# Opening layer 0 with half of the contraction: input products over half of K placed between the ada sums, gate sums behind q, rotary angles on GpSimd

## The reference

```python
mod = c_act @ w_ada[layer] + b_ada[layer]            # 6 x 1024 values
shift_m, scale_m, gate_m, shift_f, scale_f, gate_f = split(mod, 6)
h = rms_norm(x, g_mix) * (1.0 + scale_m) + shift_m
proj = h @ w_in                                      # 1024 x 1952
c_q, c_kv, k_rope, q_sb, k_sb, v_sb = split(proj)    # 256, 128, 32, 512, 512, 512
```

## Time and profile before

| | us |
|---|---|
| median of 3 runs (lowest, highest) | 1446.91 (1445.17, 1450.16) |
| the profiled execution, its time | 1443.41 |
| its span | 1441.6 |
| PE busy in the span | 1358.2 (94%) |
| DVE busy | 1261.1 (87%) |
| ACT busy | 937.8 (65%) |

### The profile page before, as it was taken

How to read it: one execution, slowest core, us unless ns; L and a number is a source line. 1 busy time by engine, 2 the same in 40 slices (tenths; PEclk the granted TensorE clock), 3 DMA queues, 4 the chain that set the end, 5 groups by cost and what they waited for, 6 DMA issues and landing times.

```text
span 1441.6 us, 18313 instructions
## 1 busy us (share of the span) xinstructions
PE 1358.2 (94%) x7090; PEld 1140.5 (79%) x7090; DVE 1261.1 (87%) x1141; ACT 937.8 (65%) x875; POOL 3.8 (0%) x35
## 2 busy tenths in 40 slices
PE   2899889999999879999999999999999999999995
PEld 2777789998987758887788888888888888888884
DVE  6878789887767778999999999989999989999997
ACT  1545443333437257887787878877787877878784
POOL 1000000000000000000000000000000000000000
PEclk9898999999899899999999999999999999999999
DMA  8973468997553129999999999999999999999992
GB/s 327 358 260 133 146 246 314 334 314 255 171 216 119 59 103 396 397 398 398 397 401 395 395 396 397 400 400 389 385 400 397 396 405 391 381 396 398 399 400 102
DMA packets 189596, 467.24 MB, mean 324 GB/s; under 512 B 8734, under 2 KB 10940, under 8 KB 175164
## 3 DMA queue, kind: packets, MB, share of 16 engines
q1 hardware_dynamic: 189500, 465.98, 86.2%
HBM read 464.90 MB, written 1.05 MB: 323 GB/s over the span
## 4 chain that ended last, share of the span: by engine, by line
PE 80%; DVE 8%; DMA 8%; ACT 3%; issue 1%; SPq 0%; DVEq 0%; ACTq 0%
PE bank L1596 16%; PE bank L1597 16%; PE bank L1598 16%; PE bank L1993 6%; PE bank L1994 6%; DMA raw<-in_w_ex_down 4%; PE bank L2036 3%; PE bank L2038 3%; PE bank L2012 3%; DMA raw<-in_w_ex_up 2%; DVE w_lo L1264 2%; DVE ring_sum L993 1%; PE bank L1639 1%; PE bank L1617 1%; PE bank L1939 1%
## 5 line engine op out<-in xcount | busy, mean ns | idle before, releaser
L1264 DVE TENSOR_TENSOR w_lo<-raw,w_hi 128x2048 fp32r<-128x2048 f32 x202 | 455.8, 2287 | 33.8 <-ACT w_hi L578 33.0
L578 ACT ACTIVATE w_hi<-raw 128x2048 fp32r<-128x2048 f32 x202 | 382.1, 1917 | 51.8 <-DMA raw<-in_w_ex_up 18.4
L554 ACT ACTIVATE w_hi<-raw 128x2048 fp32r<-128x2048 f32 (+1 forms) x54 | 102.3, 1897 | 131.2 <-PE bank L1598 118.4
L1264 DVE TENSOR_TENSOR fifth_lo<-raw,fifth_hi 128x2048 fp32r<-128x2048 f32 x67 | 153.2, 2287 | 11.9 <-ACT fifth_hi L578 11.4
L1264 DVE TENSOR_TENSOR more_lo<-raw,more_hi 128x2048 fp32r<-128x2048 f32 x67 | 153.2, 2287 | 11.3 <-ACT more_hi L578 11.0
L578 ACT ACTIVATE fifth_hi<-raw 128x2048 fp32r<-128x2048 f32 x67 | 128.4, 1916 | 22.7 <-DMA raw<-in_w_ex_gate 8.0
L578 ACT ACTIVATE more_hi<-raw 128x2048 fp32r<-128x2048 f32 x67 | 128.4, 1916 | 17.9 <-DMA raw<-in_w_ex_up 6.8
L922 DVE TENSOR_TENSOR w_lo<-raw,w_hi 128x2048 fp32r<-128x2048 f32 (+1 forms) x54 | 121.7, 2258 | 19.4 <-ACT w_hi L554 19.1
L1596 PE MATMUL bank<-h_hi,w_hi 128*128 128x256 f32 x448 | 128.1, 286 | 1.6 <-DVE gate_m L971 1.6
L1597 PE MATMUL bank<-h_lo,w_hi 128*128 128x256 f32 x448 | 126.7, 283 | 0.0
L1598 PE MATMUL bank<-h_hi,w_lo 128*128 128x256 f32 x448 | 126.7, 283 | 0.0
(11 more groups left out here) (344 smaller groups left out, 2834.7 us busy)
## 6 DMA issues: line engine op xcount, KB each, us to landing
raw<-in_w_ex_gate SPq DMA_DIRECT2D x112, 1024.0 KB, 11.9
raw<-in_w_ex_up SPq DMA_DIRECT2D x112, 1024.0 KB, 12.1
raw<-in_w_ex_down SPq DMA_DIRECT2D x112, 1024.0 KB, 12.9
raw<-in_w_ada SPq DMA_DIRECT2D x48, 1024.0 KB, 6.7
raw<-in_w_in SPq DMA_DIRECT2D x12, 1024.0 KB, 6.6
raw<-in_w_ff_gate SPq DMA_DIRECT2D x10, 1024.0 KB, 5.9
raw<-in_w_ff_up SPq DMA_DIRECT2D x10, 1024.0 KB, 5.9
raw<-in_w_ff_down SPq DMA_DIRECT2D x10, 1024.0 KB, 6.3
```

Source lines behind the costliest of these rows:

```text
L554: act_e.activation(w_hi[:, s % SPLIT, 0:words], raw[:, n % RAW, 0:words], ACT.Copy).then_inc(hi_done, 1)
L578: act_e.activation(dst, raw[:, (N0 + n) % RAW, :], ACT.Copy).then_inc(hi_done, 1)
L1264: dve.tensor_tensor(lo, raw[:, (N0 + n) % RAW, :], hi.bitcast(F32), ALU.subtract).then_inc(lo_done, 1)
```

## The change

The first eight ada units are no longer one block. Rows are now built in the order chunk 0 and chunk 2 (shift and gain of the first half of K), then chunks 1 and 3 (the second half). Only the first two rows (four units) stand ahead of the first weights. From layer 0's `w_in`, the first half of K comes for latents, v, q and k, with the four units of the other two rows between them; then the second half for latents, v and q, two gate units, `w_uq`, the second half of k, `w_ukv`, three units. ACT brings the second half of the transposed rows out unmodulated (`late_rows`) and modulates it in place later. Both wide sums for the gate stand behind the `w_ukv` product, in banks 4 and 5. `positions` is loaded ahead of the weights and the angles are made on POOL by 21 instructions. The biases of the gates are loaded later (in front of the 18th unit). Layer 1 keeps its order.

```diff
-    chunks = [(0, c) for c in range(12)] + [(1, c) for c in (0, 1, 2, 3, 6, 7, 8, 9, 4, 5, 10, 11)]
+    chunks = [(0, c) for c in (0, 2, 1, 3, *range(4, 12))] + [(1, c) for c in (0, 1, 2, 3, 6, 7, 8, 9, 4, 5, 10, 11)]
...
-    for u in ada_units[:8]:
-        add_ada(*u)
...
+        if l == 0:
+            for u in ada_units[:4]:
+                add_ada(*u)
+            add_half(w_in[l], 0, LAT, 0)
+            add_half(w_in[l], LAT + 2 * SW, SW, 0)
+            add_ada(*ada_units[4])
+            add_half(w_in[l], LAT, SW, 0)
+            add_ada(*ada_units[5])
+            add_half(w_in[l], LAT + SW, SW, 0)
+            add_ada(*ada_units[6])
+            add_ada(*ada_units[7])
+            add_half(w_in[l], 0, LAT, 1)
+            end(("lat", l), "split")
+            add_half(w_in[l], LAT + 2 * SW, SW, 1)
+            end(("v", l), "split")
+            add_half(w_in[l], LAT, SW, 1)
+            add_next_ada(2)
...
+        if l == 1:
+            add_half(w_in[l], LAT + SW, SW, 0)
+            add_next_ada(1)
+            stream.append((w_ukv[l].rearrange("(k p) n -> p k n", p=P), 1, 2 * MW, "pe"))
+            end(("ukv", l), "pe")
+            add_half(w_in[l], LAT + SW, SW, 1)
+            end(("k", l), "split")
+        else:
+            add_half(w_in[l], LAT + SW, SW, 1)
+            end(("k", l), "split")
+            stream.append((w_ukv[l].rearrange("(k p) n -> p k n", p=P), 1, 2 * MW, "pe"))
+            end(("ukv", l), "pe")
+            add_next_ada(3)
...
+            with nc.allow_non_contiguous_dma(reason="256 positions, one to a partition"):
+                sp.dma_start(pos_i[:, :], positions[0].rearrange("(g p) -> p g", p=P)).then_inc(pos_in, 16)
...
-                if n == 10:
+                if n == 17:
...
+            pool.wait_ge(pos_in, 16)
+            then(pool.tensor_copy(pos_f[:, :], pos_i[:, :]))
+            for g in range(G):
+                then(pool.tensor_scalar(ang[:, g, :], freq[:, :], pos_f[:, g:g + 1], None, ALU.mult))
...
+            for i in range(2):
+                for j, part in enumerate(TURN):
+                    src = ang[:, :, :] if j == 0 else rest[:, i, :, :]
+                    then(pool.tensor_scalar(trig[:, 0, :, :], turns[:, i, :, :], -part, None, ALU.mult))
+                    then(pool.tensor_tensor(rest[:, i, :, :], trig[:, 0, :, :], src, ALU.add))
...
+            pool.tensor_scalar(rest[:, :, :, :], rest[:, :, :, :], PI_IN, -PI_IN, ALU.min, ALU.max).then_inc(angles, 1)
+            pool.wait_ge(trig_done, 1)
...
-                act_e.wait_ge(mod_done, 4 * l + 2)
-                evacuate(m, hf, gcol(0), scol(0))
-                for _ in range(3 if l == 0 else 2):
+                    act_e.wait_ge(h_tp, 4)
+                    for j in range(2, 4):
+                        act_e.activation(hf[:, 2 * j:2 * j + 2, :], bank[j][:, :].rearrange("p (k t) -> p k t", t=T),
+                                         ACT.Copy).then_inc(late_rows, 1)
+                    act_e.wait_ge(early_mod, 2)
+                    for k in range(4):
+                        act_e.activation(hf[:, k, :], bank[k // 2][:, (k % 2) * T:(k % 2 + 1) * T], ACT.Identity,
+                                         bias=scol(0)(k), scale=gcol(0)(k)).then_inc(hf_done, 1)
                     hi(s); s += 1
-                if l == 0:
                     act_e.wait_ge(angles, 1)
                     act_e.activation(trig[:, :, :, :], rest[:, :, :, :], ACT.Sin).then_inc(trig_done, 1)
                     act_e.preload_act_table_set(EXP_LN)
-                hi(s); s += 1
-                if l == 0:
+                    for _ in range(3):
+                        hi(s); s += 1
+                    act_e.wait_ge(late_rows, 2)
+                    act_e.wait_ge(mod_done, 2)
+                    for k in range(4, KD):
+                        act_e.activation(hf[:, k, :], hf[:, k, :], ACT.Identity,
+                                         bias=scol(0)(k), scale=gcol(0)(k)).then_inc(hf_done, 1)
...
+            def first_mod(half, done):
+
+                ks = slice(4 * half, 4 * half + 4)
+                c0, c1 = 4 * half, KD + 4 * half
+                at = bank[7][:, 0:16] if half == 0 else bank[0][:, LAT:LAT + 16]
+                dve.tensor_tensor(mod[:, 0, 0, 0, ks], at[:, c0:c0 + 4], cols1[:, c0:c0 + 4], ALU.add).then_inc(done, 1)
+                link(dve.tensor_tensor(modt[:, 0, ks], at[:, c1:c1 + 4], cols1[:, c1:c1 + 4], ALU.add))
+                dve.scalar_tensor_tensor(out=mod[:, 0, 0, 1, ks], in0=modt[:, 0, ks], scalar=1.0,
+                                         in1=cols1[:, 96 + 4 * half:96 + 4 * half + 4], op0=ALU.add, op1=ALU.mult).then_inc(done, 1)
...
-            for _ in range(4):
+            for _ in range(2):
...
                 if l == 0:
+                    lo(s); s += 1
+                    dve.wait_ge(crossed, 2)
+                    first_mod(0, early_mod)
+                    split_operand(m, hf, range(2))
+                    lo(s); s += 1
+                    for _ in range(2):
+                        sum_unit()
+                        lo(s); s += 1
+                    sum_unit()
+                    sum_unit()
+                    lo(s); s += 1
                     dve.wait_ge(crossed, 4)
-                    mod_shift(0, 0, 4, 0)
-                    mod_gain(0, 0, 4, KD)
-                    lo(s); s += 1
-                    split_operand(m, hf)
+                    first_mod(1, mod_done)
+                    split_operand(m, hf, range(2, 4))
                     lo(s); s += 1
                     lo(s); s += 1
-                    rotation_angles()
+                    sum_unit()
...
-                gate_half(6, RM, gate_m, 0, gate_m[:, 0:512], 2 + l)
-                gate_half(7, RM + 1, gate_m, 1, gate_m[:, 512:1024], 2 + l)
-                lo(s); s += 1
                 if l == 0:
                     sum_unit()
+                else:
+                    gate_half(6, RM, gate_m, 0, gate_m[:, 0:512], 2 + l)
+                    gate_half(7, RM + 1, gate_m, 1, gate_m[:, 512:1024], 2 + l)
+                    lo(s); s += 1
...
+                    gate_half(4, RM, gate_m, 0, gate_m[:, 0:512], 2 + l)
+                    gate_half(5, RM + 1, gate_m, 1, gate_m[:, 512:1024], 2 + l)
+                    lo(s); s += 1
+                    sum_unit()
...
-            across(0, 4, 0)
-            across(1, 4, 4)
+            across(0, 7, 0)
             transposes(0, 2)
-            across(2, 4, 8)
-            across(3, 4, 12)
+            across(1, 7, 8)
...
+                if l == 0:
+                    rows_half(0, LAT, 0, m)
+                    pe.wait_ge(late_rows, 2)
+                    rows_half(2, 512, 0)
+                    columns_half(4, 0)
+                    across(2, 0, LAT + 4, fresh=False)
+                    columns_half(6, 0, between=lambda: across(3, 0, LAT + 12, fresh=False))
+                    rows_half(0, LAT, 1, m)
+                    rows_half(2, 512, 1)
+                    columns_half(4, 1)
...
-                across(RM + 1, 7)
-                pe.wait_ge(gate_done, 2 if l == 0 else 6)
-                columns_half(6, 0)
+                if l == 1:
+                    across(RM + 1, 7)
+                    pe.wait_ge(gate_done, 6)
+                    columns_half(6, 0)
+                else:
+                    columns_half(6, 1)
...
-                columns_half(6, 1)
+                if l == 1:
+                    columns_half(6, 1)
+                else:
+                    pe.wait_ge(qk_done, 2)
+                    across(RM, 4)
+                    across(RM + 1, 5)
+                    pe.wait_ge(gate_done, 2)
```

124 lines of the change are left out of this document (67 added, 57 removed).

## The result

The changed kernel's median is 1450.55 us over 20 runs (1445.78 to 1453.93), against 1444.51 us over 20 runs for the kernel before (1441.95 to 1450.16). The ratio is 1.0039, with a 95% interval of 1.0028 to 1.0050: slower by about 6 us, where "near nothing" was forecast. The prediction added its -0.2 us to 1446.91, the median of three runs, which lies 2.4 us above the median of all 20. So the forecast of 1446.7 was 3.9 us off in time, but the change itself was missed by 6.2 us; that 1450.55 falls inside the stated range of 1442.5 to 1450.8 is owed to the high starting value. The profiled execution took 1450.92 us, so its marks can be set beside those of the one before (1443.41).

What follows compares the result with a forecast made beforehand. PE was taken as the pace from about 45 us, with DVE's list setting attention's start. Terms -13.2 + 5.9 + 2.5 - 0.8 + 0.5 + 4.9 gave -0.2, so 1446.9 became 1446.7 us; range 1442.5 to 1450.8.

Steps and rivals of the forecast that it cites:

- The walk to U: Layer 0, first product to the end of the `w_ukv` product (U): U at 89.3, 5.1 us earlier than before.
- Behind U: From the `w_ukv` product's end to attention: DVE's fixed list takes 15.5 us instead of 10.6, so attention starts at 104.8.
- 13 us of head start: Opening of the kernel: first product at 30.2 instead of 43.37, 13.2 us earlier.
- the last rival: Start of attention: DVE's pieces behind U not on the path, attention at about U + 10, giving 1441.8 us; chance 0.05.
- a hold of 0.14 us each: Start, mild case of the POOL rival: each of 21 POOL operations holds DVE 0.14 us, costing 1.5 us, giving 1448.4.
- That rival: Start of the kernel: POOL's angles and DVE's ada sums get in each other's way, slower, at 1450 us; chance 0.1.
- the clock's term: PE's clock around layer 0's attention: low stretch merely moved, bounds +2.7 and -4.4 us, taken as zero.
- the dear bound: Attention's opening at the low clock: slower `across` and first two products, in all +2.7 us.
- The credit of up to 4.4 us: Later attention rounds: the new low stretch ends earlier, so the costliest rounds, slow before, regain up to 4.4 us.
- the clock falls ahead of attention and stays down as long as before: Rival at attention's opening: -0.2 + 2.7 us, giving 1449.4 us; chance 0.15.
- a shift at attention is carried to the end: From layer 0's attention on: the rest follows PE, so a shift of attention's start reaches the end.

Runs made afterwards that it cites:

- one sum early: Changed kernel with one `lo` and one ada unit's sum moved on DVE ahead of the `w_ukv` product's end: 1441.74 us, ratio 0.9986 to the kernel before.
- heads first: Changed kernel with both ada sums ahead of the `w_ukv` product's end and both `lo` behind the heads' copies: 1437.02 us, ratio 0.9956 to the kernel before.
- The version with POOL alone: Kernel before with only `positions` loaded first and the angles made on POOL: 1442.29 us, ratio 0.9990.
- two other versions that open low: Changed kernel with one ada sum early (1441.74 us), and changed kernel with k's second half behind `w_ukv` again (1445.72 us).
- changed again: The changed kernel rerun without edits for a second trace: 1447.95 us, ratio 1.0019 to the kernel before.
- the filling: Changed kernel plus nine unread products on PE in the gap ahead of attention: 1444.07 us, ratio 0.9998; repeated at 1443.81 us, ratio 0.9998.
- the delay experiment: Kernel before with four extra DVE copies behind layer 0's attention: 1444.81 us, ratio 0.9994.

## Why the prediction was wrong

**The walk to U was right.** First product at 29.70, forecast 30.2. U at 88.7, forecast 89.3. The wait for the second half of h is 1.45 us, forecast 1.2; the one for `lat_t` 1.34, forecast 1.3. `w_ukv` begins at 85.14, in the window 85 to 87 that was named.

**Behind U was right.** DVE idles for 5.02 us (forecast about 5), then takes 15.3 us for the list that was priced at 15.5. PE idles 8.56 us (forecast 8 to 10) and attention opens at 104.18, forecast 104.8. The versions with one sum early and with heads first show by removal that these pieces hold attention back: 4.6 and 7.5 us. The 13 us of head start were indeed lost ahead of attention, and the last rival, the head start carried whole, fell. (Two rivals' times don't follow from their own sums: a hold of 0.14 us each gives 1448.2, not 1448.4, and attention at U + 10 gives 1441.3, not 1441.8. Neither changes anything.)

**POOL was no burden.** That rival gave 1450, near the measured number, but for a reason that the trace refutes. POOL's timeline:

```profile
9.15 0.25 POOL L572 TENSOR_TENSOR rest<-trig,ang 128x32 f32<-128x32 f32 x1
...
12.03 0.74 POOL L571 TENSOR_SCALAR trig<-turns 128x32 f32<-128x32 f32 x1
12.85 0.67 POOL L572 TENSOR_TENSOR rest<-trig,ang 128x32 f32<-128x32 f32 x1
...
16.00 0.25 POOL L572 TENSOR_TENSOR rest<-trig,rest 128x32 f32<-128x32 f32 x1
16.72 0.24 POOL L574 TENSOR_SCALAR rest<-rest 128x64 f32<-128x64 f32 x1
```

And DVE's, over the same microseconds:

```profile
10.29 5.48 DVE L1071 SCALAR_TENSOR_TENSOR ring_sum<-raw,cols,ring_sum 128x512 f32<-128x512 f32 x7
```

While DVE sums, from 10.29 to 15.77, POOL's operations take 0.67 to 0.74 us instead of 0.25 to 0.29. DVE's seven slices take 5.48 us, to the hundredth what they took before in the earlier trace rows. POOL was held, DVE was not, and the angles were done at 16.96, twice as early as ACT wants them. The version with POOL alone says the same in time.
"SBUF — State Buffer" of the Trainium skill ("SBUF: two separate sides") has a DVE operation with two inputs in SBUF and a POOL operation that reads SBUF exclude each other for a whole instruction. The trace agrees in that POOL's operations were held; DVE's kept their 5.48 us, so in this case only POOL paid.

**The failed step is the clock's term.** The prediction gave bounds of +2.7 and -4.4 us and said: "I take zero, as both come from the same kind of low stretch, merely moved". The low stretch wasn't merely moved. With PE idle for 8.56 us the clock fell to 0.50, stayed there over attention's opening until about 118, and was low once more from about 122 to 125, so that the rounds further back kept part of theirs. Measured from opening to mark N, the stage takes 86.1 us in the changed kernel (and 85.6 and 87.0 in the two other versions that open low), against 82.6 and 83.4 in the kernel before and 83.0 to 84.1 in the others that open high. With the means of both groups (86.2 and 83.3) that is +2.9, where the dear bound was +2.7 and zero was taken. Attention opens about 1 us earlier (104.1 against 105.2 in the means), so about 2 us are left at mark N (190.3, 190.4, 190.0 against 187.5 and 188.8). The credit of up to 4.4 us never came, and it was priced from a low stretch at 108 to 121.7 that the second trace of the kernel before doesn't have in that place. This is the rival "the clock falls ahead of attention and stays down as long as before", which had 0.15; it named this cause, with +2.5 us for the change, which from the median of 20 gives 1447.0 and not the 1450.55 measured. The evidence for it stood in the prediction: an idle time of 8 to 10 us, and the earlier trace rows, where the clock stays low although PE is busy.
The rule that leant the other way, that work releases the clock ("TensorE: Matmul & The Clock Gate" of the Trainium skill, Part 1, "The HAM clock gate"), is not what this trace shows: PE is busy for 5.82 of 6 us from 104 to 110, and the clock is at 0.50 until about 118, 14 us after work resumed.

**A term was missing altogether.** The prediction argued that a shift at attention is carried to the end and left it at that. About 2 us at mark N don't make 6 at the end. The rest lies in low stretches further down that come in some executions only: one in layer 1's attention, with what follows it worth 4.0 us between the changed kernel's own traces, and one in the last 25 us, worth 3. The one in layer 1 is in 3 of the 5 traces of versions whose layer 0 attention opens low (changed, changed again, one sum early), and in none of the other 9. That fits a draw which is tilted by what happened in layer 0, but 14 traces don't prove it. The times of all runs say more. With 2.1 us, the shift at mark N, taken off each of the changed kernel's 31 runs, 20 of them still lie above 1447 us, against 9 of 73 runs of the kernel before; with the filling it is 2 of 21 as they stand. And within the changed kernel the 12 runs with a mean granted clock of 0.970 or more have a median of 1446.2 us, the 19 below it 1450.9. So some 3 of the 5 us between the medians of all runs lie behind mark N, and they come as a larger share of long executions, which goes away with the filling; that it is the further low stretches that make them long is read from the five traces. What carries the influence over 250 us of other work stays open; the delay experiment, meant to part a mere shift from it, shifted nothing. The one in the tail is in traces of both kernels (the first two of the changed one, the second of the one before, one sum early), and was not told apart from chance.

**The size of the loss.** The filling leaves the gap's length and DVE's list alone and keeps the clock up. With it the changed kernel is level with the kernel before (0.9998 twice), so the whole measured loss hangs on the clock in the gap, directly or through the tilt; the interval of about 0.1% leaves room for a microsecond or two either way.

## What to carry to other kernels

When an edit gives an engine's early start back as a wait, price the wait twice: by the time, and by what PE's clock does over the work behind it. Gaps of 4.0 to 8.6 us in front of a stage of small products made that stage about 3 us longer here, beside the gap itself. Look at the list of the engine that is waited for: moving four DVE pieces off the wait turned a loss of 6 us into a gain of 8, and 12 with two further waits filled and one more piece moved. Where nothing could be moved, nine products that nobody reads kept the clock up and won the loss back. Take more than one trace before a difference far down the program is read as an effect of the edit.

## What the hardware showed

- PE at 5.82 busy of 6 us did not bring the clock up between 104 and 110, in attention's rounds of fp32 products with 64 or 96 rows and 128 columns; it stood at 0.50 from about 98 to 118.
- With PE idle for 3.99, 4.07 or 8.56 us the first row behind ran at the low clock (1.84 us for eight products); with 0.82 or 0.83 us idle it ran at full clock (1.02).
- Beside DVE sums with two operands in SBUF, POOL's small operations went from 0.25 to 0.29 us up to 0.67 to 0.74 us, and DVE's did not change (5.48 us for seven in both).
- Loading `positions` ahead of everything moved DVE's first sum from 9.03 to 9.16 (three traces) to 9.51 to 9.81 (eleven traces), so by about 0.6 us; the prediction had estimated 1.2.
- Three traces of the changed kernel have spans of 1449.2, 1449.2 and 1442.1 us, the last two of them from one chip.
